# Layer step with a mixture of experts on one core: one-hot products for the first expert's rows, choice by counting, and the scatter ahead of the overflow branch

## What is computed

```python
lg = (h @ w_rg + b_rg)                      # 4 groups
g_sel = jnp.argmax(lg, axis=-1)
le_sel = take(h @ w_re + b_re, g_sel)       # 4 experts of the chosen group
vals, idx = lax.top_k(le_sel, 2)
gate = p_sel * softmax(vals)
for e in range(16):
    y = (silu(h @ w_eg[e]) * (h @ w_eu[e])) @ w_ed[e]
    out = out + gate[..., e:e + 1] * y
x = x + out
x = x + sigmoid(rmsnorm(x) @ w_ple_gate) * (p @ w_ple_proj)
```

## Time and profile before

| | us |
|---|---|
| median of 3 runs | 967.55 (966.94 to 968.12) |
| the profiled execution | 967.38 |
| its span, first to last instruction | 965.7 |
| TensorE busy | 875.8 (91%) |
| weight loads of TensorE | 754.1 (78%) |
| VectorE busy | 589.0 (61%) |
| ScalarE busy | 450.3 (47%) |
| GpSimd busy | 105.8 (11%) |
| mean granted clock of TensorE | 0.963 |

### The profile page before, as it was taken

The page is one execution under the profiler, slowest core; times in us unless marked ns, Lnnn a source line. Parts: engine busy times, 40 slices in busy tenths (PEclk is TensorE's granted clock), DMA queues, the critical chain, the costliest instruction groups (busy, mean ns, idle before and its releaser), DMA issues.

```text
span 965.7 us, 14540 instructions
## 1 busy us (share of the span) xinstructions
PE 875.8 (91%) x5215; PEld 754.1 (78%) x5215; DVE 589.0 (61%) x745; ACT 450.3 (47%) x652; POOL 105.8 (11%) x165
## 2 busy tenths in 40 slices
PE   5999999899899999999999728999999999983798
PEld 4878788688799998999878626888888877772686
DVE  5467346766435343323544616999998998894852
ACT  5312443333233332222322316888888888882431
POOL 3444710000000000000001030000000000003400
PEclk9999999999999999999999869999999999996799
DMA  8024793120446465532200589999999999997311
GB/s 308 1 88 131 229 291 94 34 77 12 145 144 215 151 199 162 165 117 87 88 0 1 202 328 343 331 390 393 393 391 394 391 392 393 392 390 267 124 44 55
DMA packets 121794, 201.61 MB, mean 209 GB/s; under 512 B 6686, under 2 KB 44222, under 8 KB 121744
## 3 DMA queue, kind: packets, MB, share of 16 engines
q1 hardware_dynamic: 113104, 170.84, 50.7%
q0 software_dynamic: 8640, 30.09, 9.1%
HBM read 173.60 MB, written 27.30 MB: 208 GB/s over the span
## 4 chain that ended last, share of the span: by engine, by line
PE 66%; DMA 9%; DVE 9%; SPq 5%; issue 5%; ACT 3%; POOL 2%; DVEq 0%; POOLq 0%; ACTq 0%
PE bank L434 19%; PE bank L436 18%; PE bank L435 18%; DMA raw<-in_w_exp_down 6%; SPq L366 5%; DVE wlo L390 3%; PE bank L1650 2%; PE bank L1817 1%; ACT whi L386 1%; PE bank L1764 1%; PE bank L1859 1%; DVE qn L1124 1%; POOL moe_rows L737 1%; PE bank L1833 1%; DMA raw<-in_w_exp_gate 1%
## 5 line engine op out<-in xcount | busy, mean ns | idle before, releaser
L390 DVE TENSOR_TENSOR wlo<-raw,whi 128x1024 fp32r<-128x1024 f32 (+1 forms) x266 | 312.9, 1191 | 137.1 <-ACT whi L386 126.8
L386 ACT ACTIVATE whi<-raw 128x1024 fp32r<-128x1024 f32 (+1 forms) x266 | 273.9, 1034 | 171.9 <-PE bank L436 136.5
L434 PE MATMUL bank<-hh,whi 128*128 128x320 f32 x448 | 142.7, 318 | 0.0
L435 PE MATMUL bank<-hh,wlo 128*128 128x320 f32 x448 | 139.0, 310 | 0.0
L436 PE MATMUL bank<-hl,whi 128*128 128x320 f32 x448 | 138.8, 310 | 0.0
L434 PE MATMUL bank<-whi,hh 128*128 128x512 f32 x280 | 113.8, 406 | 7.7 <-DVE hl L1124 5.4
L434 PE MATMUL bank<-whi,xh 128*128 128x512 f32 x256 | 103.5, 404 | 9.4 <-DVE xl L1124 5.6
L436 PE MATMUL bank<-wlo,hh 128*128 128x512 f32 x280 | 110.6, 395 | 0.0
L435 PE MATMUL bank<-whi,hl 128*128 128x512 f32 x280 | 110.5, 395 | 0.0
L436 PE MATMUL bank<-wlo,xh 128*128 128x512 f32 x256 | 101.1, 395 | 0.0
L435 PE MATMUL bank<-whi,xl 128*128 128x512 f32 x256 | 101.0, 394 | 0.0
(11 more groups left out here) (234 smaller groups left out, 1277.4 us busy)
## 6 DMA issues: line engine op xcount, KB each, us to landing
raw<-in_w_exp_gate SPq DMA_DIRECT2D x64, 512.0 KB, 11.3
raw<-in_w_exp_up SPq DMA_DIRECT2D x64, 512.0 KB, 11.6
raw<-in_w_exp_down SPq DMA_DIRECT2D x64, 512.0 KB, 12.4
raw<-in_w_in SPq DMA_DIRECT2D x40, 512.0 KB, 6.3
moe_rows<-zero POOLq DMA_DIRECT2D x16, 512.0 KB, 13.1
kc<-in_cache_k SPq DMA_DIRECT2D x16, 512.0 KB, 5.2
vc<-in_cache_v SPq DMA_DIRECT2D x8, 1024.0 KB, 5.2
xe<-moe_rows SPq DMA_DIRECT2D x16, 512.0 KB, 10.9
```

The costliest lines, as they stand in the source:

```text
L386: nc.scalar.activation(part(whi[:, u.slot], short), part(raws[u.raw], short), ACT.Copy).then_inc(s_hi, 1)
L390: nc.vector.tensor_tensor(out=part(wlo[:, u.slot], short), in0=part(raws[u.raw], short), in1=part(whi[:, u.slot], short).bitcast(F32), op= ...
L434: pe.matmul(out, a_hi, b_hi, start=first, stop=False, skip_group_check=True)
L435: pe.matmul(out, a_lo, b_hi, start=False, stop=False, skip_group_check=True)
```

## The change

- **Choice.** `ranked` replaces `top`: for each of four logits it counts those that beat it (greater, or equal and earlier), and the choice is the one with the count 0 or 1. The three maxima for the softmax are taken behind the masks. The splits of units U_M and U_M + 1 move from ahead of the choice to behind the slots, U_M + 3 to the expert's own loop.
- **Slots.** The expert's base is added to the ranks of all 16 experts first (`rke`), and one masked sum gives the slot. `slotm` holds the rows that fit; a row that doesn't goes to a place past the end (`nowhere`). `slotv` is the same for the overflow rows, `slot` the one that the gather reads.
- **First expert's rows.** A one-hot matrix `oh` (token by place, 128 places) is made from expert 0's ranks, and 40 products of `h2` with it give expert 0's rows, already transposed, in banks 4 and 5. They take the place of its load and of its eight transposes.
- **Order.** TensorE makes two tiles of the second half of the per-layer product ahead of the ranks, one behind them, and the last two behind the one-hot products; the fifth goes to bank 7 and behind the flag. GpSimd scatters by `slotm` ahead of the flag's load, the overflow rows inside the branch. SyncE issues units U_M + 8 and U_M + 9 ahead of its wait for the scatters, U_M + 10 and U_M + 11 too but behind the last per-layer tile, and of the rows only expert 1's.
- **Constants.** GpSimd makes `earlier`, `eidxc`, `places` and `nowhere` at the start, and no longer `desc`; TensorE and VectorE wait for 22 and 23 constants instead of 18 and 19.

New tiles and semaphores are left out here.

```diff
+        oh = at("oh", [P, NT, C], F32, HT.start + 8 * D * 4)
...
+        NOWHERE = NE * C + NE * OV_TILES * P
+        Xd = nc.dram_tensor("moe_rows", (NOWHERE + 2 * NT * P, D), F32, kind="Internal").ap()
...
+        def ple_bank(n, t):
+
+            return bank[7] if n == 1 and t == NT - 1 else bank[t]
...
 
@@ -561,13 +578,13 @@
             sp.wait_ge(s_rt, 1)
             for j in range(4, 8):
                 load_unit(sp, Unit(U_M + j), gate_up_src(0, j))
-            sp.wait_ge(s_scat, 16 * 2 * NT)
-            for e in range(2):
-                sp.dma_start(xe[:, e], Xd[e * C:(e + 1) * C, :]).then_inc(s_xe[e], 16)
-            sp.wait_ge(s_free, F_G)
             sp.wait_ge(s_sq, 2 * NT)
             for j in range(4):
+                if j == 2:
+                    sp.wait_ge(s_mm, 5 * (U_P + 2))
                 load_unit(sp, Unit(U_M + 8 + j), gate_up_src(1, j))
+            sp.wait_ge(s_scat, 16 * 2 * NT)
+            sp.dma_start(xe[:, 1], Xd[C:2 * C, :]).then_inc(s_xe[1], 16)
...
             over = sp.value_load(flag[0:1, 0:1], min_val=0, max_val=1)
             with sp.If(over > 0):
+                sp.wait_ge(s_scatv, 16 * 2 * NT)
...
             for tile, value in ((ident, 0.0), (identb, 0.0), (diagmask, 0.0), (before, 1.0), (onesb, 1.0), (ones1, 1.0),
-                                (mhalf, -0.5), (zero, 0.0), (spread, 0.0), (newmask, 0.0)):
+                                (mhalf, -0.5), (zero, 0.0), (spread, 0.0), (newmask, 0.0), (earlier, 1.0)):
                 pl_.memset(tile[:], value).then_inc(s_made, 1)
-            pl_.iota(desc[:], pattern=[[-1, 4]], base=4, channel_multiplier=0,
-                     allow_small_or_imprecise_dtypes=True).then_inc(s_made, 1)
             pl_.iota(eidx[:], pattern=[[1, NE]], base=0, channel_multiplier=0,
                      allow_small_or_imprecise_dtypes=True).then_inc(s_made, 1)
-            pool.wait_ge(s_made, 12)
+            pl_.iota(eidxc[:], pattern=[[C, NE]], base=0, channel_multiplier=0,
+                     allow_small_or_imprecise_dtypes=True).then_inc(s_made, 1)
+            pl_.iota(places[:], pattern=[[1, C]], base=0, channel_multiplier=0,
+                     allow_small_or_imprecise_dtypes=True).then_inc(s_made, 1)
+            pl_.iota(nowhere[:], pattern=[[P, 2], [2 * P, NT]], base=NOWHERE, channel_multiplier=1,
+                     allow_small_or_imprecise_dtypes=True).then_inc(s_made, 1)
+            pool.wait_ge(s_made, 15)
+            pl_.affine_select(out=earlier[:], in_=earlier[:], compare_op=ALU.is_gt, fill=0.0, base=0,
+                              pattern=[[1, 4], [-1, 4]], channel_multiplier=0).then_inc(s_made, 1)
...
+            def scatter(slots, done):
+                for t in range(NT):
+                    for k in range(2):
+                        pool.indirect_dma_start(out=Xd[:, :], out_offset=bass.IndirectOffsetOnAxis(
+                            ap=slots[:, k, t:t + 1], axis=0), in_=h2[:, t, :], in_offset=None).then_inc(done, 16)
+
+            pool.wait_ge(s_zero, 16 * NE)
+            pool.wait_ge(s_slotm, 1)
+            scatter(slotm, s_scat)
+
             pool.wait_ge(s_flag, 1)
             over = pool.value_load(flag[0:1, 0:1], min_val=0, max_val=1)
-            pool.wait_ge(s_zero, 16 * NE)
+            pool.wait_ge(s_slot, 1)
             with pool.If(over > 0):
                 with pool.Fori(0, NE * OV_TILES) as o:
                     pool.dma_start(Xd[bass.ds(NE * C + o * P, P), :].rearrange("r (a b) -> r a b", b=P),
                                    zero[:, None, :].to_broadcast([P, D // P, P])).then_inc(s_zero, 16)
                 pool.wait_ge(s_zero, 16 * (NE + NE * OV_TILES))
-            pool.wait_ge(s_slot, 1)
-            for t in range(NT):
-                for k in range(2):
-                    pool.indirect_dma_start(out=Xd[:, :], out_offset=bass.IndirectOffsetOnAxis(
-                        ap=slot[:, k, t:t + 1], axis=0), in_=h2[:, t, :], in_offset=None).then_inc(s_scat, 16)
+                scatter(slotv, s_scatv)
...
+            def ple_out(n, t):
+                act.wait_ge(s_mm, 5 * (U_P + n) + t + 1)
+                sc.activation(pp[:, t, n * W:(n + 1) * W], ple_bank(n, t)[:, :], ACT.Copy).then_inc(s_free, 1)
+
+            for t in range(NT):
+                ple_out(0, t)
+            hi(U_P + 4)
+            act.wait_ge(s_d, 2)
+            sc.activation(gexp[:], gdiff[:], ACT.Exp).then_inc(s_rx, 1)
+            sc.activation(vexp[:], vdiff[:], ACT.Exp).then_inc(s_rx, 1)
+            for t in range(3):
+                ple_out(1, t)
...
             rows_hi(0)
+            for t in range(3, NT):
+                ple_out(1, t)
+            hi(U_P + 5)
...
-            lo(U_M)
-            lo(U_M + 1)
...
+            def ranked(logits):
+
+                mine = logits[:, :, :, None].to_broadcast([P, NT, 4, 4])
+                other = logits[:, :, None, :].to_broadcast([P, NT, 4, 4])
+                tt(beats[:, :, :, 0], other, mine, ALU.is_gt)
+                link(tt(beats[:, :, :, 1], other, mine, ALU.is_equal))
+                link(tt(beats[:, :, :, 1], beats[:, :, :, 1], earlier[:, None].to_broadcast([P, NT, 4, 4]), ALU.mult))
+                link(ve.tensor_reduce(out=order_[:], in_=beats[:], axis=AX.XY, op=ALU.add))
 
             dve.wait_ge(s_rt, 1)
             link(tt(lg[:], bank[6][:, 0:NT * (NG + NE)].rearrange("p (t n) -> p t n", t=NT),
                     rbias[:, None, :].to_broadcast([P, NT, NG + NE]), ALU.add))
-            top(lg[:, :, 0:NG], gmax, og[:])
-            tt(gdiff[:], lg[:, :, 0:NG], bc(gmax, NG), ALU.subtract).then_inc(s_d, 1)
+            ranked(lg[:, :, 0:NG])
+            link(ve.tensor_scalar(og[:], order_[:], 0.0, None, ALU.is_equal))
             link(tt(prod[:], lg[:, :, NG:].rearrange("p t (g j) -> p t j g", g=NG),
                     og[:, :, None, :].to_broadcast([P, NT, EG, NG]), ALU.mult))
             link(ve.tensor_reduce(out=lsel[:], in_=prod[:], axis=AX.X, op=ALU.add))
-            top(lsel[:], v1, ok[:, 0])
-            link(ve.scalar_tensor_tensor(out=lsel2[:], in0=ok[:, 0], scalar=-3.0e38, in1=lsel[:], op0=ALU.mult,
-                                         op1=ALU.add))
-            top(lsel2[:], v2, ok[:, 1])
-            tt(vdiff[:], v2[:], v1[:], ALU.subtract).then_inc(s_d, 1)
+            ranked(lsel[:])
+            for k in range(2):
+                ins = ve.tensor_scalar(ok[:, k], order_[:], float(k), None, ALU.is_equal)
+            link(ins)
             for k in range(2):
                 ins = tt(Mk[:, k].rearrange("p t (g j) -> p t g j", g=NG), og[:, :, :, None].to_broadcast([P, NT, NG, EG]),
                          ok[:, k, :, None, :].to_broadcast([P, NT, NG, EG]), ALU.mult)
             link(ins)
             tt(Mb[:], Mk[:, 0], Mk[:, 1], ALU.add).then_inc(s_M, 1)
-
+            tt(Mf[:], Mk[:, 0], Mk[:, 1], ALU.add)
+            ve.tensor_reduce(out=gmax[:], in_=lg[:, :, 0:NG], axis=AX.X, op=ALU.max)
+            ve.tensor_reduce(out=v1[:], in_=lsel[:], axis=AX.X, op=ALU.max)
+            link(tt(lsel2[:], ok[:, 1], lsel[:], ALU.mult))
+            tt(gdiff[:], lg[:, :, 0:NG], bc(gmax, NG), ALU.subtract).then_inc(s_d, 1)
+            link(ve.tensor_reduce(out=v2[:], in_=lsel2[:], axis=AX.X, op=ALU.add))
+            tt(vdiff[:], v2[:], v1[:], ALU.subtract).then_inc(s_d, 1)
+
+            dve.wait_ge(s_rk, 1)
+            link(ve.tensor_copy(rk[:], bank[6][:, P:P + NT * NE].rearrange("p (t e) -> p t e", t=NT)))
+            for t in range(NT):
+                ve.tensor_scalar(oh[:, t], places[:], rk[:, t, 0:1], Mf[:, t, 0:1], ALU.is_equal, ALU.mult).then_inc(s_oh, 1)
+
+            ve.tensor_scalar(over_row[:], rk[:], float(C), float(2 * NOWHERE), ALU.is_ge, ALU.mult)
+            link(tt(rke[:], rk[:], eidxc[:, None, :].to_broadcast([P, NT, NE]), ALU.add))
+            link(tt(rke[:], rke[:], over_row[:], ALU.max))
+            link(tt(mr[:], Mk[:], rke[:, None].to_broadcast([P, 2, NT, NE]), ALU.mult))
+            link(ve.tensor_reduce(out=slotf[:, 0], in_=mr[:], axis=AX.X, op=ALU.add))
+            tt(slotm[:], slotf[:, 0], nowhere[:], ALU.min).then_inc(s_slotm, 1)
+
+            link(ve.tensor_scalar(slotf[:, 1], slotf[:, 0], float(NOWHERE), None, ALU.is_ge))
+            ve.tensor_reduce(out=ovm[:], in_=slotf[:, 1], axis=AX.XY, op=ALU.max).then_inc(s_ovm, 1)
+            link(tt(mr[:], Mk[:], rk[:, None].to_broadcast([P, 2, NT, NE]), ALU.mult))
+            link(ve.tensor_reduce(out=slotf[:, 2], in_=mr[:], axis=AX.X, op=ALU.add))
+            link(tt(mr[:], Mk[:], eidx[:, None, None, :].to_broadcast([P, 2, NT, NE]), ALU.mult))
+            link(ve.tensor_reduce(out=slotf[:, 3], in_=mr[:], axis=AX.X, op=ALU.add))
+            link(ve.scalar_tensor_tensor(out=slotf[:, 2], in0=slotf[:, 3], scalar=float(T - C), in1=slotf[:, 2],
+                                         op0=ALU.mult, op1=ALU.add))
```

(72 more changed lines are left out.)

42 lines of the change are left out of this document (18 added, 24 removed).

## The result

The changed kernel took 954.47 us (median of 4 runs, 953.38 to 955.37) where the kernel before, on the same chip, took 967.84 (4 runs, 966.94 to 969.08): 13.4 us less, a ratio of 0.9868 [0.9845, 0.9891]. The forecast was 951.8 in a range of 946 to 959.5. The profiled execution took 954.69 us (span 953.1 and 1.59 around it) against 967.38.

The account below looks back on a forecast made before the run. The expert stage was taken as bound by its transfers, held up by a full weight ring. Last landing -15.7 us and start +0.1 gave -15.6 from the profiled 967.38: 951.8 us, range 946 to 959.5 for 8 in 10.

Parts of the forecast that it names:

- 80 records of one-hot products: TensorE, expert 0's rows: 40 fp32 products as 80 records at 0.112 us, 8.9 us at full clock, 546.7 to 555.6.
- scatters landed: GpSimd's ten scatters: last landing at 568.8 us, bounds 566 and 572, moving the sum one for one.
- expert 1's gate: TensorE's first gate product of expert 1 near 575.5 us, 19.4 us earlier than before.
- last down unit landed: End of the expert stage's transfers: 209 blocks, 279.9 us, plus remainder 2.2 from 569.7; 851.8 against 867.5, 15.7 us earlier.
- tail: After the last down unit lands: 98.2 us, not touched by the change.
- The first rival: TensorE's start sets the whole: transfers keep up, the gain is expert 1's 19.4 us, 948.1 us; chance 0.12.
- the ring: Rival: the 12-unit weight ring fills if expert 1 starts after 584.5; 7.6 us stay lost, 959.4 us; chance 0.2.
- the slow clock: One-hot products at TensorE's slow clock: 10.2 us more, expert 1 near 585.7, just enough to fill the ring.
- nothing gained: Rival: expert 1's rows hold TensorE as expert 0's did, the ring gives back the rest: 967 us; chance 0.04.
- units 10 and 11 take two blocks, 2.7 us: Two weight units loaded amid the scatters share their engines, moving the scatters' landing by 2.7 us, to 568.8.
- the 0.1 us of delay in the forecast: Kernel start: GpSimd's extra constants take some 0.7 us, 0.1 left on the path; bounds 0 and 0.7.
- likeliest case: The prediction's own case: transfers run through without a full ring, 951.8 us, range 949 to 955; chance 0.6.

Follow-up runs that it names:

- experiment 1: Changed kernel with only the one-hot products undone, expert 0's rows loaded and transposed again behind the scatters: 967.15 us, ratio 1.0001 to the kernel before.
- 6: Changed kernel without the low-by-high product in experts 3 to 14, a third of TensorE's products there: 954.61 us, ratio 0.9872 to the kernel before.
- 7: Changed kernel loading only 512 of 1024 columns of the rows of experts 3 to 15, on all 128 partitions: 944.84 us.
- experiment 2: Changed kernel with the scatters again behind the flag and the branch's value load, all else kept: 960.99 us, ratio 0.9928 to the kernel before.
- experiment 3: Changed kernel with weight units 10 and 11 issued behind expert 1's rows: 953.06 us, ratio 0.9842 to the kernel before.
- experiment 9: Changed kernel with weight units 10 and 11 issued only when eight of ten scatters have landed: 953.04 us, ratio 0.9869 to the kernel before.
- experiment 11: The kernel before, unchanged, profiled a second time for its tail: 967.8 us, tail 98.1 us.
- number 8: Changed kernel with expert 1's rows by one-hot products too and units 12 to 15 ahead of the wait for the scatters: 952.43 us.

## Why the prediction was right, and where its terms were off

Beside each step of the forecast what the profile shows, as time behind R (before: R = 540.36, changed: 538.00):

| step | forecast | measured |
|---|---|---|
| Mb written | R+4.1 | R+4.2 |
| main slots written | R+7.8 | R+8.4 |
| first scatter | R+8.3 | R+9.3 |
| 80 records of one-hot products | 8.9 us, clock 1 | 9.09 us, clock 1.00 |
| expert 0's first product | R+18.0 | R+18.6 |
| scatters landed | R+28.4 | R+31.1 |
| from there to expert 1's gate | 6.8 | 6.85 |
| expert 1's gate | R+35.1 | R+37.9 |
| last down unit landed | R+311.4 | R+314.9 |
| tail | 98.2 | 100.2 |

- **The mechanism is the one forecast.** Expert 1 starts in time, so the ring is never full, the transfers run through, and they set the end. Shown: by experiment 1 (expert 0 late again, ring full again, nothing left of the gain), by 6 (a third of TensorE's products less: the same time) and by 7 (half of a row block less: 9.6 us). TensorE's gaps begin early, as forecast: from 650 to 800 us it is busy for 145.0 us, where it was 148.4. From 570.0, when expert 1's rows begin to flow, to 852.93 are 283 us, against the forecast's 279.9+2.2 = 282.1. The first rival, TensorE's start (948.1), falls by 6; the ring (959.4) didn't fill, neither here (expert 1 at R+37.9) nor in experiment 2 (R+44.0), but did in experiment 1, where expert 0 itself starts only at R+37.0; the slow clock didn't come to the one-hot products, though it did to expert 1's transposes behind the 4.88 us of idle time (1.97 us for eight), as before; "nothing gained" is what experiment 1 measured, without the one-hot products.
- **The step that was off: the scatters' landing, by 2.7 us** (1.9 to 2.7 over the four profiles with this code). One of them is the start: five one-hot tiles took 1.37 us, not 1.0, and the first scatter came 0.9 behind the slots, not 0.5 (and the choice 0.1). The other 1.7 us are the term "units 10 and 11 take two blocks, 2.7 us". It priced the two units at the loads' full rate of 392 GB/s. From 549 to 568 scatters and loads together ran at 330 GB/s, and without the two units the last scatter lands 4.1 to 4.8 us sooner (experiment 3), not 2.7. The scatters don't reach the loads' rate by themselves either: from 556 to 567 in the kernel before, with nothing else under way, they run at 357 GB/s (experiment 3). That the splits lengthen the scatters' issue was seen, and lies in this number too. Why the rate falls further with loads among them stays open: experiment 9, which moved the units by a few scatters, gained nothing.
- **The tail, called unchanged, grew by 1.9 us.** The change touches none of its code. Three gathers are held by 2.2 us in all by an add that runs when they start (experiment 11's rows). Read from the traces only: I made no kernel that sets this order, and number 9, which has the changed kernel's tail and the short gathers (tail 96.7), says that the order is not tied to the change. I take it to hang on a few tenths of a microsecond in the arrival of rows, which no run shows. Not all of the short tail of number 9 is behind the first gather: that one starts 14.6 us behind the last landing there, 15.8 in the changed kernel.
- **The front** gave 2.4 us in the profiles that no step claims. R is 540.4 and 540.6 in the two profiles of the kernel before, 537.4 to 539.1 in ten with the changed front, and 540.5 in one more with that same front (number 8). So the same instructions take either time; why the changed kernels mostly take the shorter is open. At the start itself TensorE's first transposes come at 8.29 us (before 8.35), and the 0.1 us of delay in the forecast can't be found.
- **Sum.** The forecast's -15.7 is -12.2 as measured; with +1.9 in the tail and -2.4 in the front the profiles differ by 12.7. Of the 3.5 missing in it 2.7 are the landing, 0.8 the stream behind. The total is 2.7 us off (954.47 against 951.8), inside the likeliest case's own range of 949 to 955. In part that is luck: the front and the tail, which no step has, nearly cancel, and without both it would be 967.38-12.2 = 955.2.
- **A sentence to correct.** The prediction set the 1.81 us of one scatter against the Trainium skill ("SBUF — State Buffer", "Who interferes with whom"), for its inference that a tensor_tensor doesn't stop descriptors being written. The same section also says that a VectorE instruction with two inputs in SBUF contends with a GpSimd instruction that reads SBUF, and that whoever issues first holds the shared ports for its whole instruction. An indirect transfer's instruction reads its slots there (that this is the read that counts is my reading). With that three of the rows agree. The scatter at 559.65 meets the second of three splits, which runs until about 560.7: 1.1+0.95 against 1.96 measured. The one at 552.67 meets a split that ends at 553.50: 0.8+0.95 against 1.65. The one at 554.63 runs beside a difference from a PSUM bank (`xl<-bank,xh`, 553.92 to 555.19), with one input in SBUF, and takes 0.95. A fourth row doesn't follow from the page: the scatter at 558.39 starts 0.02 us behind a split (558.37) and still takes 0.95. Nor is VectorE held in turn: the splits take 1.21 to 1.28 us each, beside scatters or not.

## What to carry to other kernels

Ask of an early load whether its buffer's user also comes early: here the early scatter alone was worth nothing, the early first expert alone some 6 us, both together 13, because what pays is a stream that never stops. When a stage is bound by its transfers, a microsecond saved ahead of it counts only if the stream begins earlier to run without a gap, and more transfers put into a quiet stretch are paid for by the ones that share it. If a transfer has to be cut, try its columns first and not its partitions: half the columns cost half a block here, half the partitions more than a whole one.
